# A two-layer mixer and a five-branch block on one NeuronCore: a new order of the opening, split logits of the forgetting heads, and gate products between them

## The reference, cut to what matters

```python
def first_block(x, c, positions, mod_w, mod_b, ...):
    for l in range(DEPTH):                                   # 2 layers
        mod = c @ mod_w[l] + mod_b[l]                        # 1024 -> 6 * 1024
        sh1, sc1, g1, sh2, sc2, g2 = [m[:, None, :] for m in jnp.split(mod, 6, axis=-1)]
        h = _rmsnorm(x, norm1_g[l]) * (1.0 + sc1) + sh1
        x = x + g1 * _mixer(h, ...)
        h = _rmsnorm(x, norm2_g[l]) * (1.0 + sc2) + sh2
        x = x + g2 * _conv_ffn(h, ...)
    return _rmsnorm(x, final_g)

def _forgetting_attention(q, k, v, log_f):                   # 8 heads of 64
    cum = jnp.cumsum(log_f, axis=1)
    ...
        logits = jnp.einsum("bqhd,bshd->bhqs", qb, k).astype(jnp.float32) * scale
        logits = logits + jnp.moveaxis(cq, 1, 2)[..., None] - cum_k[:, :, None, :]
        logits = jnp.where(causal[None, None], logits, NEG_INF)
        p = jax.nn.softmax(logits, axis=-1).astype(v.dtype)
```

## Time and profile before

| | |
|---|---|
| median of 3 runs | 1714.79 us (1713.35 to 1715.84) |
| the profiled execution, its time | 1720.28 us |
| its span, first to last instruction | 1718.5 us |
| TensorE busy | 1589.4 us, 92% |
| VectorE busy | 1139.0 us, 66% |
| ScalarE busy | 822.8 us, 48% |
| mean granted clock of TensorE | 0.943 |

### The profile page before, as it was taken

One profiled execution on the slowest core, in us unless ns is written; L12 is line 12 of the kernel. 1 busy time (PEld: TensorE's weight loads), 2 busy tenths in 40 slices (PEclk: granted clock), 3 DMA queues, 4 the chain that ended last, 5 costly groups with the idle time before them and its releaser, 6 DMA issues. The chain is left out here.

```text
span 1718.5 us, 31556 instructions
## 1 busy us (share of the span) xinstructions
PE 1589.4 (92%) x12784; PEld 1499.6 (87%) x12784; DVE 1139.0 (66%) x2133; ACT 822.8 (48%) x1496; POOL 59.4 (3%) x64
## 2 busy tenths in 40 slices
PE   4799999899988999998999989899999698999997
PEld 2687899899987878998999979899999598998997
DVE  2556446788634663467987686967777559677874
ACT  3353444555434434445555564464445553644453
POOL 1000000000010000000000110000000200000001
PEclk8797999999998978999999999999999899999999
DMA  9443355456463533553664544244345432443430
GB/s 394 167 161 149 145 195 184 149 219 215 174 269 144 199 142 128 198 196 129 240 221 180 189 165 154 99 172 148 123 159 185 147 123 75 172 155 140 154 142 25
DMA packets 42048, 288.89 MB, mean 168 GB/s; under 512 B 4624, under 2 KB 6672, under 8 KB 7472
## 3 DMA queue, kind: packets, MB, share of 16 engines
q1 hardware_dynamic: 38880, 280.83, 44.1%
q10 hardware_dynamic: 3024, 6.03, 1.0%
HBM read 284.75 MB, written 2.10 MB: 167 GB/s over the span
## 5 line engine op out<-in xcount | busy, mean ns | idle before, releaser
L1819 DVE TENSOR_TENSOR w_lo<-ring,w_hi 128x1024 fp32r<-128x1024 f32 x436 | 527.6, 1232 | 331.1 <-ACT w_hi L1496 330.2
L1213 PE MATMUL bank<-h_hi,w_hi 128*128 128x256 f32 x2256 | 643.3, 292 | 12.6 <-ACT h_hi L1552 8.5
L1214 PE MATMUL bank<-h_hi,w_lo 128*128 128x256 f32 x2256 | 633.8, 288 | 0.0
L1219 PE MATMUL bank<-h_lo,w_hi 128*128 128x256 f32 x2256 | 584.4, 288 | 0.0
L1496 ACT ACTIVATE w_hi<-ring 128x1024 fp32r<-128x1024 f32 x436 | 447.6, 1053 | 102.3 <-PE bank L1219 101.9
L1213 PEld LDWEIGHTS bank<-h_hi,w_hi 128*128 128x128 f32 x2256 | 445.0, 197 | 24.2 <-issue 20.9
L1214 PEld LDWEIGHTS bank<-h_hi,w_lo 128*128 128x128 f32 x2256 | 445.1, 197 | 0.5 <-issue 0.5
L1219 PEld LDWEIGHTS bank<-h_lo,w_hi 128*128 128x128 f32 x2256 | 415.5, 197 | 0.0
L1251 PE MATMUL bank<-w_hi,h_hi 128*128 128x256 f32 (+1 forms) x304 | 88.7, 297 | 16.3 <-DVE w_lo L1819 12.7
L1213 PE MATMUL bank<-a_hi,w_hi 128*128 128x256 f32 x352 | 100.4, 285 | 0.5 <-DVE w_lo L1819 0.5
L1214 PE MATMUL bank<-a_hi,w_lo 128*128 128x256 f32 x352 | 99.2, 282 | 0.0
(11 more groups left out here) (326 smaller groups left out, 2397.5 us busy)
## 6 DMA issues: line engine op xcount, KB each, us to landing
ring<-weights SPq DMA_DIRECT2D x266, 1024.0 KB, 4.9
pos_bias<-scratch ACTq DMA_DIRECT2D x4, 512.0 KB, 4.7
x<-x_t ACTq DMA_DIRECT2D x1, 1024.0 KB, 6.2
scratch<-line ACTq DMA_DIRECT2D x1, 1024.0 KB, 5.1
mem_x<-mem_t ACTq DMA_DIRECT2D x1, 1024.0 KB, 7.0
out_t<-x SPq DMA_DIRECT2D x2, 512.0 KB, 2.6
co<-const SPq DMA_DIRECT2D x1, 461.5 KB, 6.7
levels_f<-levels ACTq DMA_DIRECT2D x1, 448.0 KB, 13.3
```

The costliest lines, as they stand in the source:

```text
L1213: pe.matmul(to, WH[:, b % SPLIT, o, :], hi[:, k, :], start=(i == 0), stop=False)
L1214: pe.matmul(to, WL[:, b % SPLIT, o, :], hi[:, k, :], start=False, stop=False)
L1219: last = pe.matmul(to, WH[:, b % SPLIT, o, :], lo[:, k, :], start=False, stop=(i == n - 1))
L1819: ve.tensor_tensor(WL[:, b % SPLIT], ring_half(b), WH[:, b % SPLIT].bitcast(F32), ALU.subtract).then_inc(w_lo_v, 1)
```

## The change

In the opening the scale (`g` = 1) comes before the shift, each part is reduced right after its product (`modred` for two of the eight columns), the norm's values are made in a step `vals` of their own after the root, and the chunks of blocks 0 to 3 are loaded and split ahead of the last two parts of the shift. The setup's tables are made one pair of products earlier than its products. The forgetting heads' q and k are split into high and low parts (ScalarE writes the high part, VectorE the low one and frees the bank), their logits are three fp32r products, and the bias is one fp32r product over 32 rows. Two of four gates that stood elsewhere go between the pairs of heads. `h_val` gives up its own memory and shares that of q and k.

```diff
-    for g in (0, 1):
+    for g in (1, 0):
         for part in range(4):
             mod(0, g, part)
-        if g == 0:
+            shifted = p.full_bank()
+            p.add("modred", ps=shifted, l=0, g=g, part=part, after=state["parts"][-1:])
+        state.update(summed=None, parts=[])
+        if g == 1:
             root(x_stats, "mod")
-        reduce_mod()
+            p.add("vals", mode="mod", l=0, which=0, hn=0, src="x")
...
-        norm("mod", None, "x", x_stats, rooted=l == 0, l=l, which=0)
+        norm("mod", None, "x", x_stats, rooted=l == 0, l=l, which=0,
+             early=shifted if l == 0 else None)
...
         p.together(firsts.pop("tm"))
+        if l == 0:
+            p.add("setup_tables")
         ev = ev + pair("tm", qi[2:4], what="qi", q=1)
...
-        f0 = att("fox", l, 0, 8, P, 0, qk, v_taken)
-        gate(), gate()
-        f1 = att("fox", l, 1, 8, 2 * P, 1, qk, v_taken)
+        f0 = att("fox", l, 0, 8, P, 0, qk, v_taken, [gate, None, gate, None])
+        f1 = att("fox", l, 1, 8, 2 * P, 1, qk, v_taken, [gate, None, gate, None])
         att_out(f0, [gate, gate, gate])
         s0 = att("sparse", l, 0, 8, P, 0, turned_a, ev[:2])
         att_out(f1, [gate, gate, gate])
...
-        att_out(s0, [gate, gate, gate])
+        att_out(s0, [gate, gate])
         ots.append(att_turn(f1, 4))
-        att_out(s1, [gate, gate, gate])
+        att_out(s1, [gate, gate])
...
-        st.upto = min(st.first + SPLIT, len(p.blocks)) - 1 if begun else 1 if st.kind == "norm" else -1
+        first_ones = st.kind == "mod" and st.g == 0 and st.part >= 2 or st.kind == "norm"
+        st.upto = min(st.first + SPLIT, len(p.blocks)) - 1 if begun else 3 if first_ones else -1
...
-                for j in range(KD):
+                for j in red_cols(st):
                     m = pe.matmul(to[:, j:j + 1], modacc[:, j // 2, (j % 2) * P:(j % 2 + 1) * P], ones[:, 0:1],
...
                 for e, h in enumerate(pair_heads(st.hp)):
                     o = to[:, e * S:e * S + st.W]
-                    m = pe.matmul(o, q(h), k(h), start=True, stop=(st.name != "fox"))
                     if st.name == "fox":
-                        m = pe.matmul(o, lhs16[:, h, st.t * P:st.t * P + P], rhs16[:, 0:st.W], start=False, stop=True)
+                        (qh, ql), (kh, kl) = q(h), k(h)
+                        pe.matmul(o, qh, kh, start=True, stop=False)
+                        pe.matmul(o, qh, kl, start=False, stop=False)
+                        pe.matmul(o, ql, kh, start=False, stop=False)
+                        m = pe.matmul(o, lhs32[:, h, st.t * P:st.t * P + P], rhs32[:, 0:st.W], start=False, stop=True)
+                    else:
+                        m = pe.matmul(o, q(h), k(h), start=True, stop=True)
...
+                    if st.early is not None:
+                        wait_taken(act, st.early)
                     for k in HI_ORDER:
...
-                to = qf if st.what == "q" else kf
+                to = QH if st.what == "q" else KH
                 act.activation(to[:, st.j, :], bank[st.ps.bank][:, 0:S], ACT.Copy,
-                               scale=0.125 if st.what == "q" else 1.0).then_inc(taken[st.ps.bank], 1)
+                               scale=0.125 if st.what == "q" else 1.0).then_inc(qk_hi, 1)
...
+            def vals(st):
+                v, hi, lo, rs, gain = output_of(st)
+                own.wait()
+                for k in range(KV):
+                    ve.scalar_tensor_tensor(v[:, k, :], src_of(st.src)[:, k, :], gain(k)[0], rs[:], ALU.mult,
+                                            ALU.mult).then_inc(hval_v, 1)
...
-                own.inc(ve.scalar_tensor_tensor(lf16[:, :, 0:8], fx[:], 0.0, fln[:], ALU.min, ALU.subtract))
-                ve.scalar_tensor_tensor(lf16[:, :, 8:16], fx[:], 0.0, fln[:], ALU.min,
-                                        ALU.subtract).then_inc(decay_ready, 1)
+                for r in range(4):
+                    m = ve.scalar_tensor_tensor(lf32[:, :, r, :], fx[:], 0.0, fln[:], ALU.min, ALU.subtract)
...
-                f = bank[st.ps.bank][0:16, 0:S]
+                f = bank[st.ps.bank][0:32, 0:S]
...
+                step(ve.tensor_copy(cum_h[:], f))
+                step(ve.scalar_tensor_tensor(cum_x[:], cum_h[:].bitcast(F32), co[0:32, low:low + 1], f, ALU.mult, ALU.add))
...
                 for h in range(8):
-                    m = ve.tensor_scalar(lhs16[:, h, :], f, co[0:16, l0 + h:l0 + h + 1], co[0:16, l0 + 8 + h:l0 + 9 + h],
-                                         ALU.mult, ALU.add)
+                    m = ve.tensor_scalar(lhs32[:, h, :], cum_x[:], co[0:32, l0 + h:l0 + h + 1],
+                                         co[0:32, l0 + 8 + h:l0 + 9 + h], ALU.mult, ALU.add)
...
+            def qkf(st):
+                if st.l == 0 and st.what == "q" and st.j == 0:
+                    ve.wait_ge(line_out, 16)
+                low, high, scale = (QL, QH, 0.125) if st.what == "q" else (KL, KH, 1.0)
+                ve.wait_ge(qk_hi, 8 * st.l + (4 if st.what == "k" else 0) + st.j + 1)
+                ve.scalar_tensor_tensor(low[:, st.j, :], bank[st.ps.bank][:, 0:S], scale, high[:, st.j, :].bitcast(F32),
+                                        ALU.mult, ALU.subtract).then_inc(taken[st.ps.bank], 1)
```

More of the change, by code:

```diff
@@ L106, in __init__ @@
         self.scale, self.lag, self.dir, self.prevn, self.k0, self.k1, self.ys = scale, lag, dir, prevn, k0, k1, ys
-        self.gate, self.sc_taken, self.last_ready, self.group = gate, sc_taken, last_ready, group
+        self.gate, self.sc_taken, self.last_ready, self.group, self.early = gate, sc_taken, last_ready, group, early
 class Plan:
@@ L211, in some_mod, with att @@
             mod(l, g, part)
-    def att(name, l, t, H, W, slot, after, values):
+    def att(name, l, t, H, W, slot, after, values, mid=()):
         a = p.count("att")
@@ L221, in att @@
                   after=after if hp == 0 else [])
+            if mid and mid[hp]:
+                mid[hp]()
         p.add("ex", name=name, l=l, t=t, H=H, W=W, slot=slot, a=a, hs=hs)
@@ L744, in constants @@
     for h in range(8):
-        lhs[8 + h, h] = 1.0
-        lhs[h, 8 + h] = 1.0
+        lhs[[16 + h, 24 + h], h] = 1.0
+        lhs[[h, 8 + h], 8 + h] = 1.0
     put("sel_lhs", lhs)
+    low = np.zeros((P, 1), np.float32)
+    low[8:16], low[24:32] = -1.0, -1.0
+    put("sel_lo", low)
     lev = np.zeros((P, 7, P), np.float32)
@@ L890, in program @@
         R = place("rot", [P, NT, 20, DH], 0)
-        lhs16 = place("lhs16", [16, 8, S], 0)
+        hb = place("h_val", [P, KD, S], 72960)
+        lhs32 = place("lhs32", [32, 8, S], 0, F32R)
         OH = place("o_hi", [P, 8, S], 0, F32R)
@@ L1093, in heads_q @@
             if st.name == "fox":
-                return (lambda h: qf[half(h), h // 2, t * P:t * P + P], lambda h: kf[half(h), h // 2, 0:W],
+                return (lambda h: [m[half(h), h // 2, t * P:t * P + P] for m in (QH, QL)],
+                        lambda h: [m[half(h), h // 2, 0:W] for m in (KH, KL)],
                         lambda k, h: Vf[:, k, h * DH:h * DH + DH])
@@ L1118, in add_square, with red_cols @@
                                  ALU.add).then_inc(sq_sum, 1)
+        def red_cols(st):
+            return range(KD) if st.part is None else range(2 * st.part, 2 * st.part + 2)
         def src_of(name):
@@ L1318, in cum @@
                 pe.wait_ge(decay_ready, st.l + 1)
-                pe.matmul(to[0:16, 0:P], lf16[:, 0, :], upto1[:, 0:P], start=True, stop=True)
-                pe.matmul(to[0:16, P:S], lf16[:, 0, :], upto1[:, P:2 * P], start=True, stop=False)
-                pe.matmul(to[0:16, P:S], lf16[:, 1, :], upto1[:, 0:P], start=False, stop=True).then_inc(ready, 1)
+                lf = [lf32[:, t].rearrange("p r h -> p (r h)") for t in range(NT)]
+                pe.matmul(to[0:32, 0:P], lf[0], upto1[:, 0:P], start=True, stop=True)
+                pe.matmul(to[0:32, P:S], lf[0], upto1[:, P:2 * P], start=True, stop=False)
+                pe.matmul(to[0:32, P:S], lf[1], upto1[:, 0:P], start=False, stop=True).then_inc(ready, 1)
             def idx(st):
@@ L1849, in bounds, with setup_tables @@
                 own.wait()
-            def setup(st):
+            def setup_tables(st):
                 ve.wait_ge(setup_in, 64)
@@ L1879, in setup @@
                 ve.tensor_scalar(ang[:, 4:6], ang[:, 4:6], 3.141592, -3.141592, ALU.min, ALU.max).then_inc(angle, 1)
+            def setup(st):
                 for h, u in enumerate(st.e):
@@ L1890, in modred @@
                 wait_ready(ve, st.ps)
-                tt(modv[:, st.l, st.g, :], bank[st.ps.bank][:, 0:KD], ss(("mod_b", st.l, st.g), 0, KD),
+                j = slice(red_cols(st).start, red_cols(st).stop)
+                tt(modv[:, st.l, st.g, j], bank[st.ps.bank][:, j], ss(("mod_b", st.l, st.g), 0, KD)[:, j],
                    ALU.add).then_inc(taken[st.ps.bank], 1)
@@ L1894, in modred @@
                 if st.g in (1, 4):
```

(13 more changed lines are left out.)

39 lines of the change are left out of this document (24 added, 15 removed).

## The result

The changed kernel takes 1687.89 us (median of 4 runs, 1681.08 to 1692.26), the kernel before 1715.32 us beside it: a ratio of 0.9838 (95% interval 0.9803 to 0.9873), 27.4 us less. 1685.8 was forecast. The profiled execution took 1686.78 us, its span is 1684.7, 33.8 less than that of before, whose profiled execution was 5 us slower than its median.

The account below looks back on a forecast made before the run. TensorE, busy for 92% of the span, was taken as the bound, through its work, waits and clock. Terms 8.9 + 8.0 + 14.4 - 2.3 = 29.0 us took the median 1714.79 to 1685.8, range 1678 to 1694.

Parts of the forecast that it names:

- Part A: Opening, from the shift's last parts to the first product: first product at 38.8 against 47.69, 8.9 us won.
- Part B: Setup to end of q products: wait gone, products at full clock, sum 10.3, 2.3 taken back for clock falls: 8.0 us.
- Part C: Fox stretches of both layers: wait ahead, new heads, gates and clock falls together win 6.5 + 7.9 = 14.4 us.
- Part D: Small additions: more VectorE operations in `decay2` and `cum`, one gate fewer in `att_out`, later v products: 2.3 us lost.
- chunk 8 from 31.55 to 34.9: Opening: product, copy and reduction of a shift part at low clock, started at 31.55 and done by 34.9.
- Its wait goes: Setup: TensorE's wait of 4.45 us for the table `rel_rep` disappears, as tables are made under the first products.
- Only the splits for the pair after next stand behind it: Setup: VectorE has no other work where the tables are made; only later splits come after them.
- the clock, 6 us a layer: Fox stretches: about two clock falls in each layer, 3 us each.
- Rival 2: Fox heads: the constant 0.20 us belongs to fp32 products, not changed rows; 1673 with falls, 1659 without; chance 0.1.
- rival 4: Fox stretches: mixing gates and logits holds the clock low; 1735 if wholly low; chance 0.05.
- rival 1: Whole change: the clock stays up everywhere, 43.3 us won, 1671.5; chance 0.2.
- rival 3: Opening gives half, through late table DMAs or a slower shift chain: 1696.4; chance 0.18.

Follow-up runs that it names:

- e1: The opening's part of the change alone, on the kernel before, forgetting heads as before: 1703.64 us, ratio 0.9925.
- e4: Split fp32r logits and moved gates of the forgetting heads, on the kernel before, opening as before: 1698.23 us, ratio 0.9899.
- e7: Changed kernel with the scale's parts reduced at once behind the root and the shift's third copy ahead of splitting blocks 2 and 3: 1684.8 us.
- e6: Changed kernel with the setup's tables made ahead of the first group of products instead of behind it: 1683.58 us, ratio 0.9816.
- e5: Changed kernel with the bias product over 64 rows, in the same half as the head's q and k: 1670.89 us, ratio 0.9744.
- e10: Kernel before, fp32 logits and gates unmoved, only the bias product widened from 16 to 64 rows in the head's half: 1691.18 us, ratio 0.9862.
- e11: Kernel before with split fp32r logits and the bias product over 64 rows in the head's half, gates and opening as before: 1696.36 us.
- e9: Changed kernel with the edits of e5 and e6: 1665.03 us, ratio 0.9709.

## Why the prediction was right, and which terms were not

The total is right, 1685.8 against 1687.89, and so are the mechanisms in the main: e1 and e4 show that the opening and the heads both gain. That it is right to 2 us is in part luck. By profile 1691.3 was forecast and 1686.78 measured, so the traces' gain was forecast 4.5 us too small: A and B came out smaller, C larger, and 2.5 us were won outside them where D had 2.3 lost. Against that stands that the trace of the kernel before was 5 us slower than its median and that of the changed kernel 1.1 faster; the forecast took a trace's gain off a median.

- **Part A, 8.9 us forecast, 5.5 measured** (6.5 in the changed kernel's second trace). The step that failed is "chunk 8 from 31.55 to 34.9": it starts the chain at the chunk's landing. TensorE was not there yet: it began this part at 32.74 and ended its reduction at 37.27. I charged the chain of product, copy and reduction to the last two parts only; it holds for all, 3.4 us a part in the first four, and the root's six products behind them took 2.77 us, against 1.46 in e7. And the four `w_hi` stood in ScalarE's order ahead of the copy, 1.87 us. e7 takes both away and has its first product at 38.63, near the 38.8 forecast. The terms of A add up to 39.0 at low clock and 37.2 at full, not to 39.2 and 37.6.
- **Part B, 8.0 forecast, 4.3 measured, and 8.0 in the second trace.** "Its wait goes" failed in both: 1.44 us stayed. "Only the splits for the pair after next stand behind it" had the order the wrong way round; the splits stand ahead. In the first trace the clock was low through the setup as before, in the second it was not. Without the wait (e6) B would be 10.7 on the first trace's scale, near the 10.3 of the sum without the 2.3 taken back.
- **Part C, 14.4 forecast, 21.5 measured.** The wait ahead was 2.40 (2.9 forecast), heads 0.73 and 0.86 (0.85 and 0.88): some 3 us in both layers. The other mis-sized term is the clock, 6 us a layer. A clock of 0.84 over 33.01 us is 10.6 us low; 0.89 over 31.52 is 6.9 low. The prediction had low-clock work take half the time at full clock, which is too much: the starts in a gate are 0.213 and 0.12 apart, so low time loses 44% and not half, here 4.6 and 3.0 us, and a gate costs 2.2 us more at low clock and not 2.9. That most of C is clock was right: by the same 44% the old stretches had lost 12 and 13 us, so some 18 of the 21.5 are clock.
- **Part D, 2.3 lost.** It can't be told apart from the clock. In layer 0 it is 12.52 us instead of 10.88 from the start of the wait for `lf` to the products of 256 columns with `qi_t`, but the wait itself is only 0.16 longer; the rest is a fall of the clock, of the kind that the kernel before had in layer 1.
- **The rule on the change of rows.** The Trainium skill, page TensorEngine Tiling, section Key Properties, has it that a change of tiling mode drains TensorE. e5 and e10 agree: 15.0 and 25.9 us for making the rows equal. The prediction priced it in the new heads, and took from it that the narrow heads win nothing; it did not draw the other conclusion, that the rows alone were the fault. Nor did it see what its own row of the sparse heads says beyond that: 0.26 us for 256 columns is less than the 0.43 that four cycles a column make, so heads in different halves overlap where the rows don't change. Rival 2 (cheap switches) is refuted by the gaps, rival 4 (clock held low) by 0.84 and 0.89, rival 1 (always up) by the same numbers. For rival 3, half an opening, e1 speaks in part: it gives 10.7 us, between the forecast's 16.9 and the rival's 9, both before small losses.

## What to carry to other kernels

When small accumulating products cost much more than their columns say, compare them with a stream of the same products without the small partner: here 0.2 us a product went at the changes between 64 and 16 rows, and the overlap of heads in different halves was lost with it; padding the narrow product with zero rows to the shape and half of its partner was worth about as much as the split into faster products, new buffers and a new order together. A step moved earlier in a common list brings its lookahead work along: look at what each engine does ahead of it at the new place. In a chain of product, copy and reduction on TensorE count every link, not the last ones. And before you price a stretch from one trace, look at a second trace of the same program.

## What the runs showed of the hardware

With equal rows 16 fp32 products of 128 columns took 2.72 us, 0.17 each, less than the 0.21 that four cycles a column make at 2.4 GHz: heads in the two halves of the rows overlap, as the rows of e11 show. The clock is in part a draw. Windows of the changed kernel, the wait for `lf`, the small products behind it and the group after these, layer 0 and then layer 1:

```profile
93.50:96.65 3.15, 0.00 (x0) 0.03 (x1) 2.70 (x6) 2.46 (x5) 0.00 (x0) 1.00 0.38 161
96.65:99.11 2.46, 2.46 (x22) 2.04 (x22) 1.54 (x5) 0.66 (x2) 0.00 (x0) 0.76 0.71 233
99.11:106.09 6.98, 6.98 (x51) 6.85 (x50) 5.08 (x16) 1.04 (x3) 0.00 (x0) 0.84 0.17 70
558.92:562.08 3.16, 0.01 (x1) 0.03 (x1) 2.70 (x6) 2.47 (x5) 0.00 (x0) 1.00 0.42 174
562.08:565.60 3.52, 3.52 (x22) 2.76 (x22) 1.99 (x6) 0.66 (x2) 0.00 (x0) 0.52 0.76 272
565.60:571.62 6.02, 6.02 (x51) 5.88 (x50) 4.64 (x14) 1.04 (x3) 0.00 (x0) 1.00 0.04 15
```

The clock fell in both layers, for some 3.4 us each, but not at the same instructions: in layer 1 right behind the wait, in layer 0 more than a microsecond later. In the kernel before it fell in layer 1 and not at all in layer 0, where the 9.92 us behind the wait are:

```profile
106.27:116.19 9.92, 9.92 (x87) 8.99 (x87) 7.47 (x18) 3.63 (x8) 0.00 (x0) 1.00 0.33 107
```

So one and the same wait of 2.99 us was followed by a fall in one layer and by none in the other. The changed kernel's runs spread over 12 us, e9's over 2. That e9 has fewer places where the clock can fall is only argued; e4 and e10, with the opening as before, spread over less than 2 as well, and e7 over 19.
